# Hybrid decoder layer: the MLP's first up products in a new order, the norm weight put into the activations, first weights asked for sooner

## The reference

```python
h = h + rmsnorm(mix, norm_mix_post)
f = jnp.square(jax.nn.relu(rmsnorm(h, norm_mlp_pre) @ w_mlp_up)) @ w_mlp_down   # 1024 -> 4096 -> 1024
h = h + rmsnorm(f, norm_mlp_post)

def rmsnorm(x, w):
    y = x * lax.rsqrt(jnp.mean(jnp.square(x), axis=-1, keepdims=True) + 1e-6)
    return y * w
```

## Time and profile before

| | us |
|---|---|
| median of 3 runs | 1576.49 (1573.24 to 1577.84) |
| profiled execution | 1577.22 |
| its span, first to last instruction | 1575.4 |
| PE busy | 1537.2 |
| DVE, ACT, POOL busy | 1061.1, 684.6, 849.1 |
| mean granted TensorE clock | 0.991 of full |

### The profile page before, as it was taken

How to read it: one execution, slowest core, us unless ns; L and a number is a source line. 1 busy time by engine, 2 the same in 40 slices (tenths; PEclk the granted TensorE clock), 3 DMA queues, 4 the chain that set the end, 5 groups by cost and what they waited for, 6 DMA issues and landing times.

```text
span 1575.4 us, 22595 instructions
## 1 busy us (share of the span) xinstructions
PE 1537.2 (98%) x7951; PEld 1319.7 (84%) x7951; DVE 1061.1 (67%) x1617; ACT 684.6 (43%) x1329; POOL 849.1 (54%) x746
## 2 busy tenths in 40 slices
PE   8999999999999999999999997999999999999997
PEld 8999998878888888788887886788888788888885
DVE  4856516256766767677778779866666567747776
ACT  5322212144544444566664452444444445444542
POOL 7534444155777646943321428888888224405553
PEclk9999999999999999999999998999999999999999
DMA  6454622236555455699978641444444597636666
GB/s 214 113 144 122 171 54 67 67 89 178 158 169 168 138 152 170 228 334 322 327 274 294 253 128 56 141 146 154 152 154 154 201 349 242 203 104 197 188 199 147
DMA packets 225795, 280.63 MB, mean 178 GB/s; under 512 B 21401, under 2 KB 148225, under 8 KB 225697
## 3 DMA queue, kind: packets, MB, share of 16 engines
q1 hardware_dynamic: 224688, 275.69, 54.0%
q0 software_dynamic: 1008, 3.67, 1.3%
HBM read 180.63 MB, written 98.66 MB: 177 GB/s over the span
## 4 chain that ended last, share of the span: by engine, by line
PE 84%; POOL 5%; DVE 5%; DMA 2%; issue 1%; ACT 1%; SPq 1%; DVEq 0%; POOLq 0%; ACTq 0%
PE ps L2960 19%; PE ps L2951 13%; PE ps L825 7%; PE ps L884 6%; PE ps L2899 4%; PE ps L2823 4%; PE ps L1799 4%; PE ps L1785 2%; PE ps L1768 2%; PE ps L840 2%; PE ps L856 2%; PE ps L1716 2%; PE ps L1738 2%; PE ps L458 1%; PE ps L2928 1%
## 5 line engine op out<-in xcount | busy, mean ns | idle before, releaser
L2960 PE MATMUL ps<-dw_hi,df_hi 128*128 128x512 f32 x448 | 176.5, 394 | 5.4 <-DVE dw_lo L3632 5.4
L2960 PE MATMUL ps<-dw_lo,df_hi 128*128 128x512 f32 x448 | 176.0, 393 | 0.0
L2960 PE MATMUL ps<-dw_hi,df_lo 128*128 128x512 f32 x448 | 175.7, 392 | 0.0
L178 POOL TENSOR_TENSOR ring<-stage,zero 128x512 fp32r<-128x512 f32 (+2 forms) x75 | 83.6, 1115 | 152.2 <-DMA stage<-w_in 48.8
L3627 DVE TENSOR_TENSOR df_lo<-df_raw,df_hi 128x512 fp32r<-128x512 f32 x112 | 121.7, 1086 | 47.6 <-ACT df_hi L3267 47.3
L2960 PEld LDWEIGHTS ps<-dw_hi,df_hi 128*128 128x128 f32 x448 | 85.1, 190 | 23.9 <-issue 6.2
L3632 DVE TENSOR_TENSOR dw_lo<-dw_raw,dw_hi 128x512 fp32r<-128x512 f32 x96 | 80.7, 840 | 35.6 <-ACT dw_hi L3276 23.8
L3267 ACT ACTIVATE df_hi<-df_raw 128x512 fp32r<-128x512 f32 x112 | 70.3, 627 | 77.5 <-DMA df_raw<-d_f 77.0
L180 POOL TENSOR_TENSOR ring<-stage,ring 128x512 fp32r<-128x512 f32 (+2 forms) x75 | 100.5, 1340 | 5.9
L2960 PEld LDWEIGHTS ps<-dw_hi,df_lo 128*128 128x128 f32 x448 | 85.2, 190 | 18.0
L2960 PEld LDWEIGHTS ps<-dw_lo,df_hi 128*128 128x128 f32 x448 | 85.2, 190 | 17.7
(11 more groups left out here) (542 smaller groups left out, 4557.7 us busy)
## 6 DMA issues: line engine op xcount, KB each, us to landing
df_raw<-d_f SPq DMA_DIRECT2D x112, 256.0 KB, 2.7
d_f<-fa SPq DMA_DIRECT2D x105, 256.0 KB, 2.1
dw_raw<-w_mlp_down SPq DMA_DIRECT2D x96, 256.0 KB, 3.0
landA<-w_mlp_up SPq DMA_DIRECT2D x52, 256.0 KB, 3.9
stage<-w_in SPq DMA_DIRECT2D x40, 256.0 KB, 2.7
stage<-w_out SPq DMA_DIRECT2D x28, 256.0 KB, 4.2
xt<-x SPq DMA_DIRECT2D x8, 512.0 KB, 7.7
d_xT<-xdT SPq DMA_DIRECT2D x8, 512.0 KB, 3.3
```

Of the source, the lines that this page charges most:

```text
L178: pool.tensor_tensor(hi, src, k.zero[:, 0:1].broadcast_to([P, width]), ALU.add).then_inc(k.sem(fam + "_hi"), 1)
L2960: mm = pe.matmul(ps[:, base + t, :], F_AT[q % SLOTS][a][:, P * t:P * t + P], W_AT[q % SLOTS][b][:, :], start=(fresh and (a, b) == (0, 0)), ...
```

## The change

1. **Norm weight.** `high_tile` and `low_tile` multiply by the norm weight's column while they read PSUM. A column belongs to 128 rows of the transposed tile, so each instruction of 128x512 becomes four of 128x128. The multiplications of the weights go: `scaled`, the one in `early_cut`, and the column operands of `up_cuts`.
2. **Order of the first products.** PE does A11 and A12 of sub-group 0 and of sub-group 1 first (they need no table), then the other products of 0, then S1, S2, S4, S3 of 1, then A11 of 2, A22 of 1, and from there in the old order. The lists of ACT, DVE and POOL and the counts that are waited for follow: the weight highs of sub-group 0 come before `first_relu(0)` and before `first_relu(2)`, those of A11 and A12 of sub-group 1 before `first_relu(3)`; POOL makes the sums of sub-group 1 after `first_sums`. Buffers of sub-group 1 change places.
3. **First weights.** SP asks for the four quarters of sub-group 0 before the store of the last h tile. For sub-group i + 2 it waits for the fourth sum of i + 1 as well.
4. **T1's high** waits for table step 3 instead of the last step (and, as before, for the middle of up bank 7).
5. **Down products.** The cuts of tiles 0 and 1 come before the last relu (ACT) and the last square (DVE) of sub-group 13.

```diff
@@ what PE does, and in what order
-        for i in range(STEPS):
-            for n in range(7):
-                product(i, n)
+    FLOW = [(0, "A11"), (0, "A12"), (1, "A11"), (1, "A12")] + [(0, q) for q in ("S1", "S2", "S4", "S3", "A22")]
+    FLOW += [(1, q) for q in ("S1", "S2", "S4", "S3")] + [(2, "A11"), (1, "A22")] + [(2, q) for q in PRODUCTS[1:]]
+    FLOW += [(i, q) for i in range(3, STEPS) for q in PRODUCTS]
+        for i, q in FLOW:
+            product(i, q)
@@ SP, in the loop over tiles, before store_h(t)
+            if t == LAST:
+                sp.wait_ge(sem("v_cut"), HALF - EARLY)
+                load_quarter(0, "A11")
+                load_quarter(0, "A22")
+                sp.wait_ge(sem("m_mm"), len(UNITS))
+                load_quarter(0, "A21")
+                load_quarter(0, "A12")
@@ SP, loads of i + 2
+                sp.wait_ge(sem("x_raw"), 4 * (i + 1) + 4)
                 sp.wait_ge(sem("x_plo"), 4 * (i + 1) + 1)
@@ GpSimd
-        def weights_begun(i):
...
+        def weight_sums(i):
...
+                pool.wait_ge(sem("m_weighted"), len(FUSED))
             if i == 1:
                 pool.wait_ge(sem("v_up"), UP)
+            if i >= 2:
+                pool.wait_ge(sem("v_up"), sub_end(i - 2))
...
-        weights_begun(0)
-        weights_ended(0)
-        weights_begun(1)
+        weight_sums(0)
+        weight_lows(0, PLOWS)
+        weight_lows(1, PLOWS[:1])
         first_sums(fb, 6, 0)
         first_sums(fa, 8, 4)
-        weights_ended(1)
+        weight_sums(1)
+        weight_lows(1, PLOWS[1:])
@@ ScalarE
-                act.activation(HM[0][:, 4 * c:4 * c + 4, P * t:P * t + P], ps[:, TURN_BANKS[t % 2][c], :].rearrange("p (a b) -> p a b", b=P),
-                               ACT.Copy).then_inc(sem("m_hi"), 1)
+                for j in range(4):
+                    mm = act.activation(HM[0][:, 4 * c + j, P * t:P * t + P], ps[:, TURN_BANKS[t % 2][c], P * j:P * j + P], ACT.Copy,
+                                        scale=col(k, "mlp", 4 * c + j))
+                mm.then_inc(sem("m_hi"), 1)
...
+            act.wait_ge(sem("x_tstep"), 8 + c - 1 if n == 0 else 16)
...
+        weights_high(0, "A22", "S1", "A11")
         first_relu(0)
         first_relu(1)
         high_tile(NT - 2)
+        weights_high(0, "S2", "S3", "A12", "S4")
         first_relu(2)
         high_tile(NT - 1)
-        weights_high(0, *HIGHS[:4])
-        first_relu(3)
-        weights_high(0, *HIGHS[4:])
-        for n in range(4, 7):
+        weights_high(1, "A11", "A12")
+        for n in range(3, 7):
             first_relu(n)
...
-            for n in range(4):
+            for n in range(3):
                 relu(i, n)
+            if not more:
+                act.wait_ge(sem("fresh"), 2)
+                down_high(0)
+                down_high(1)
+            relu(i, 3)
@@ VectorE
+                for j in range(4):
+                    hi, lo = (x[:, 4 * c + j, P * t:P * t + P] for x in HM)
+                    mm = dve.scalar_tensor_tensor(lo, ps[:, TURN_BANKS[t % 2][c], P * j:P * j + P], col(k, "mlp", 4 * c + j), hi.bitcast(F32),
+                                                  ALU.mult, ALU.subtract)
...
             summed_tile(i, 1)
             summed_tile(i, 2)
+            if not more:
+                dve.wait_ge(sem("fresh"), 2)
+                down_low(0)
+                down_low(1)
             squared(i, 3)
             summed_tile(i, 3)
...
         first_square(5)
+        weight_low(1, "A12")
         table_step(6)
```

More of the change, by code:

```diff
@@ L2516, in down_w @@
             sp.dma_start(W_RAW[q % SLOTS][:, :], down_q[g, j, c]).then_inc(sem(f"w_in{q % SLOTS}"), 16)
[L2518 to L2523, removed]
         for u in range(2):
@@ L2669, in weights_ended @@
             if i == 1:
                 pool.wait_ge(sem("v_up"), UP)
-                pool.wait_ge(sem("f_sent1"), 16 * len(F_KEPT))
-            pool.wait_ge(own, 8 * i + 5)
-            pool.tensor_tensor(sums[i % 2]["S3"][:, :, :], unsplit(i, "A11")[:, :, :], unsplit(i, "A21")[:, :, :], ALU.subtract).then_inc(own, 1)
-            scaled(i, "A12")
-            pool.wait_ge(own, 8 * i + 7)
-            pool.tensor_tensor(sums[i % 2]["S4"][:, :, :], unsplit(i, "A12")[:, :, :], sums[i % 2]["S2"][:, :, :], ALU.subtract).then_inc(own, 1)
@@ L2677, in weights_ended @@
-            for q in ("A11", "S1", "S2", "S4"):
-                pool.wait_ge(sem("x_hi"), 7 * i + HIGHS.index(q) + 1)
+            if i >= 2:
+                pool.wait_ge(sem("v_up"), sub_end(i - 2))
+            s1, s2, s3, s4 = (sums[i % 2][q][:, :, :] for q in ("S1", "S2", "S3", "S4"))
+            a11, a12, a21, a22 = (unsplit(i, q)[:, :, :] for q in ("A11", "A12", "A21", "A22"))
+            pool.tensor_tensor(s1, a21, a22, ALU.add).then_inc(own, 1)
+            pool.wait_ge(own, 4 * i + 1)
@@ L2679, in weights_ended, with weight_lows @@
+            pool.tensor_tensor(s2, s1, a11, ALU.subtract).then_inc(own, 1)
+            pool.tensor_tensor(s3, a11, a21, ALU.subtract).then_inc(own, 1)
+            pool.wait_ge(own, 4 * i + 2)
+            if i == 1:
+                pool.wait_ge(sem("f_sent1"), 16 * len(F_KEPT))
+            pool.tensor_tensor(s4, a12, s2, ALU.subtract).then_inc(own, 1)
+        def weight_lows(i, names):
+            for q in names:
+                pool.wait_ge(sem("x_hi"), 7 * i + highs(i).index(q) + 1)
                 hi, lo = mats[i % 2][q]
@@ L2932, in up_bank, with product @@
             mm.then_inc(sem("v_up"), 1)
-        def product(i, n):
-            q = PRODUCTS[n]
+        def product(i, q):
+            n = PRODUCTS.index(q)
             bank = sub_bank(i, BANK_OF[q])
-            low, at = LOWS[q]
-            pe.wait_ge(sem(low), EACH_LOW[low] * i + at + 1)
-            if q == "A11":
-                pe.wait_ge(sem("v_sq"), (6, 8)[i] if i < 2 else UP + 4 * (i - 1))
+            low, made = low_made(i, q)
+            pe.wait_ge(sem(low), made)
+            if i < 2 and q in ("A11", "S1", "A12"):
+                pe.wait_ge(sem("v_sq"), {"A11": (3, 7), "S1": (4, 8), "A12": (5, 7)}[q][i])
+            elif q == "A11":
+                pe.wait_ge(sem("v_sq"), UP + 4 * (i - 1))
             if i == 0 and q in ("S1", "S2", "S3", "A22"):
@@ L3250, in on_scalar @@
             if more:
-                weights_high(i + 1, "A22", "S1", "A11")
+                weights_high(i + 1, *(("A22",) if i == 0 else ("A22", "S1", "A11")))
             if i:
                 kept(i, 1)
-            if more:
+            if i == 0:
+                weights_high(1, "S1", "S2", "S3", "S4")
+            elif more:
                 weights_high(i + 1, "S2", "S3")
@@ L3495, in weight_low @@
         def weight_low(i, q):
-            dve.wait_ge(sem("x_hi"), 7 * i + HIGHS.index(q) + 1)
+            dve.wait_ge(sem("x_hi"), 7 * i + highs(i).index(q) + 1)
             hi, lo = mats[i % 2][q]
```

121 lines of the change are left out of this document (63 added, 58 removed).

## The result

The changed kernel takes 1566.19 us (median of 5 runs, 1564.96 to 1568.02), the kernel before beside it on the same chip 1574.40 (1571.24 to 1577.84). The ratio is 0.9945, 95% interval 0.9929 to 0.9960: 8.7 us faster by the ratio, 6.3 to 11.2. The forecast was 1563.9 with a range of 1559.5 to 1569.5, and the measured time lies in that range. The profiled execution took 1566.74 us, its span is 1564.8.

A forecast was written before the change was run, and what follows sets the result against it. PE bounds the kernel; 17.5 us lost in sub-group 0 from VectorE's delays. Less new losses 1.7 + 0.8 + 2.3 + 1.5 leaves 11.2, plus 1.4 at the down products: 12.6 us, so 1563.9 us, range 1559.5 to 1569.5.

The forecast's parts named there:

- the table-free products: After the up banks: four products keep PE busy 11.0 us, so the gaps of 1.9 and 6.7 us go.
- VectorE's table steps 2 to 6: VectorE's table work after tile 7: alone, without GpSimd on the port, at 1.17 us a half step.
- A22's gap: PE's wait before sub-group 0's A22 for VectorE's second sum: 2.3 us, plus 1.5 for the clock.
- the down gap: PE's wait at the first down product: 3.45 us before, 2.1 after, 1.4 us won; the clock dips as before.
- the steady products: Sub-groups 2 to 13: PE is already full, so GpSimd's four fewer operations per sub-group change 0.
- ScalarE's piece: A 128x128 activation with column operand at the norm-weight exit: 0.257 us each, +1.0 us a tile.
- VectorE's pieces: Four 128x128 PSUM subtractions with column operand: 0.95 us against 0.60 for one whole, +0.7 us a tile.
- the first quarters: Sub-group 0's four weight loads asked for sooner: data near 926.5, GpSimd's sums 5 us, cost 0 on SP's queue.
- A: Rival: bank 4 does not wait, as pieces overlap better or hn(7) is not pushed; 1561.4 us; chance 0.20.
- B: Rival: GpSimd late for sub-group 1, first squares or old fb stores late; 1569.4 us; chance 0.16.
- C: Rival: products don't run ahead, PE stands in sub-group 1's A11 or A12; 1573 us; chance 0.08.
- D: Rival: after the gap before bank 4, 96 matmuls stay at 1.2 GHz, 19 us; 1582 us; chance 0.06.

The follow-up runs named there:

- x5: Changed kernel with ScalarE's seven weight highs of sub-group 0 moved behind tile 7, VectorE's order as it was: 1564.05 us, ratio 0.9928 to the kernel before.
- x2: Changed kernel with one 128x512 copy and one subtraction per half tile again, norm weight left out of the computation: 1559.97 us, ratio 0.9905 to the kernel before.
- x6: Changed kernel with GpSimd's four early sums of sub-group 0 waiting until hn(7) is written: 1563.50 us, ratio 0.9933 to the kernel before.
- x3: Changed kernel with PE's products in the old order in all 14 sub-groups: 1567.77 us, ratio 0.9958 to the kernel before.
- x8: Changed kernel with four moves: x1, x5, x7, and down cuts one tile sooner still: 1557.23 us, ratio 0.9887 to the kernel before.
- x4: Changed kernel with the cuts of down tiles 0 and 1 back behind the last relu and square: 1568.05 us, ratio 0.9962 to the kernel before.
- x7: Changed kernel with T4's highs ahead of ScalarE's second kept tile, totals 0 and 1 ahead of VectorE's two weight lows: 1562.76 us, ratio 0.9925 to before.
- x14: x10 plus two moves: VectorE's third total behind the second, ScalarE's copy of sub-group 1's A11 ahead of the relus: 1558.75 us, ratio 0.9892 to before.
- x10: x8's four moves, but the first three weight highs stay in place and only four go behind tile 7: 1555.99 us, ratio 0.9875 to the kernel before.
- x1: Changed kernel with VectorE's statistics of h tile 7 before table step 0: 1560.68 us, ratio 0.9920 to the kernel before.
- x12: Changed kernel with sub-group 0's quarter loads asked for behind the last store of h, as before the change: 1564.05 us, ratio 0.9926 to before.

## Why the prediction was nearly right

**Where it was right.** The mechanism of the table-free products (no gap at T1, none at `fb`), VectorE's table steps 2 to 6 alone at 2.35 us (step 1 took 2.89, step 7 beside GpSimd 4.52), A22's gap (2.3 forecast, 2.07 measured) with about eight slow matmuls, the down gap (2.1; 2.12), and no cost in the steady products. ScalarE's piece: eight occupy it from 941.51 to 943.51, 0.25 us each, against 0.257 from the earlier trace rows. By the Trainium skill's rule (ScalarE: Activation LUTs, "What ACT_TABLE_LOAD costs") it would be 0.293; here the row was the better source. VectorE's pieces take 0.27 each, not 0.24: +1.0 us a tile and not +0.7.

**The step that failed** is the one on the first quarters: "Its four sums take 5 us and are over before VectorE's table steps begin." The data came at 928.4 and not at 926.5, the sums took 7.1 us and not 5, and they lay on h(7), on table step 0 and so on the statistics behind it. I had costed the earlier request at nothing against SP's queue and had not asked what GpSimd's earlier start would collide with. hn(7) ended at 939.1 for a forecast 934.3 (0.9 of the difference is the later start of bank 0). The chain behind it, 10.4 us to bank 4, is exactly the forecast's; that a whole 3.6 us of this chain are highs that nobody needs yet (x5) I did not see either.

**By stretch**, forecast and measured: bank 0 to 4, 25.6 and 29.6 us; to A22, 47.3 and 48.0 (1.6 us of clock, not 0.8: PE is busy 45.9 us in this stretch, and 44.3 in x2 and x6, where no matmul was slow); to the down products, 250.7 and 249.3; from there, 320.1 and 318.0. The +4.0 was mostly hidden by 3.5 us behind A22, which I had left as before: fewer slow matmuls above all (PE's busy time in the last stretch fell by 2.8 us, of the same 1344 matmuls). Thirteen were slow at its start before and eight after; at a second wait late in it eight were slow before, after 1.96 us, and none after, after 2.11. The second of these is luck: nothing in the change aims at it. Counted from bank 0 in the two traces, 12.6 us were forecast and 11.4 measured, but by the ratio of the runs it is 8.7, and 12.6 lies outside its interval of 6.3 to 11.2. The executions of one kernel differ by 2 to 7 us, and the one profiled before (1577.22) was among the slower ones, so the sum started with gaps and slow matmuls that the median execution has less of. The time came nearer than the gain did, by luck: the forecast was taken off 1576.49, and the kernel before had 1574.40 beside the changed one. From that base the same sum gives 1561.8.

**The rivals.** A: bank 4 did wait. B and C: no product waited for its weights. D: the clock fell for seven or eight matmuls after the new gap, 1.6 us and not 19.

## What to carry to other kernels

An engine that gets its data sooner also runs sooner: look at what the other engine on its port does at that time, and what stands behind that in its order. Where a wait is put down to the last link of a chain, walk the lists of the engines ahead of it for entries that nobody needs yet; here four small moves were worth as much as the change itself. And a gap that goes leaves the next one in line: after four moves the waits were short and everywhere, and two moves more won nothing.

## What the runs showed of the hardware

A slow matmul is one at the clock's lower level (granted clock 0.5, 1.2 GHz): 0.43 us from its start to the next and not 0.23. Past the first 15 us of the kernel, no matmul of these traces was slow after a wait of TensorE under 1.9 us. Above that the length of the wait does not decide. The plainest pair is the first down product, after the same wait of 2.12 us: x3 first, then the changed kernel.

```profile
1250.46 0.47 PE L2969 MATMUL ps<-dw_hi,df_hi 128*128 128x512 f32 x1 [2.12 <-DVE dw_lo L3557]
1250.77 0.40 PE L2969 MATMUL ps<-dw_lo,df_hi 128*128 128x512 f32 x1
```

```profile
1246.82 0.52 PE L2971 MATMUL ps<-dw_hi,df_hi 128*128 128x512 f32 x1 [2.12 <-DVE dw_lo L3559]
1247.13 0.63 PE L2971 MATMUL ps<-dw_lo,df_hi 128*128 128x512 f32 x1
```

No matmul was slow after 1.94 (x8), 2.06 (x4, before A22), 2.12 (x3 and x7), 2.87 (x6, bank 4) and 3.09 us (x14). Six to nine were slow after 1.93 (before), 1.98 (x10), 2.07 and 2.12 (changed), 2.76 (x1), 3.45 (x4) and 6.23 us (x5), and thirteen after the same 3.45 us in the kernel before. They came at once in some (x12: the first row 0.80 us) and only after two or three matmuls at full speed in others (the changed kernel after 949.53). At 0.2 us each that is 1.2 to 2.6 us. The granted clock differs between executions of one kernel too: the four of x10 had 0.996, 0.999, 0.996 and 0.997 of full, and took 1557.42, 1554.77, 1557.22 and 1554.53 us. So a run of this kernel carries a few us that these orders did not decide. The Trainium skill (TensorE: Matmul & The Clock Gate, Part 1) says of the matmuls at a kernel's start that the count of slow ones varies from run to run of one kernel. The rows here are of waits in the middle of a kernel, one trace for each kernel; they show the count varying after waits of like length, and say nothing of a kernel's start.
